# One-core transformer block: the conditioning product moved from TensorE in attention to VectorE multiply-adds under the output projection and the first feed-forward

## The reference

```python
mod = silu(c) @ ada_w + ada_b            # 1024 -> 9216 = 3 sublayers x (shift, scale, gate) x 1024
h = rms_norm(x, g) * (1 + scale) + shift
x = x + 0.5 * gate * swiglu(h)           # sublayer 0, and 2; sublayer 1 has a token mixer and a whole gate
```

## Time and profile before

| | us |
|---|---|
| median of 3 runs | 1898.52 |
| lowest and highest | 1898.12, 1898.67 |
| span of the profiled execution | 1896.2 |
| PE busy | 1868.0 (99%) |
| DVE busy | 996.8 (53%) |
| ACT busy | 817.9 (43%) |
| POOL busy | 123.8 (7%) |

### The profile page before, as it was taken

The page is one execution under the profiler, slowest core; times in us unless marked ns, Lnnn a source line. Parts: engine busy times, 40 slices in busy tenths (PEclk is TensorE's granted clock), DMA queues, the critical chain, the costliest instruction groups (busy, mean ns, idle before and its releaser), DMA issues.

```text
span 1896.2 us, 22387 instructions
## 1 busy us (share of the span) xinstructions
PE 1868.0 (99%) x8923; PEld 1450.5 (76%) x8923; DVE 996.8 (53%) x1778; ACT 817.9 (43%) x1328; POOL 123.8 (7%) x148
## 2 busy tenths in 40 slices
PE   8999999999999999999999999999999999999997
PEld 6566666666788788888886777778888878888886
DVE  6667666666544653333346667845434763333322
ACT  6566656656633342222323655434432442222221
POOL 0111111110001000000010011000000100000000
PEclk9999999999999999999999999999999999999999
DMA  5444343432233232222333323221123323233331
GB/s 199 164 145 156 144 145 145 145 145 101 78 129 117 67 111 100 93 96 94 100 86 125 99 70 106 68 94 35 45 89 111 124 92 102 94 100 97 92 95 61
DMA packets 56526, 201.95 MB, mean 107 GB/s; under 512 B 6478, under 2 KB 6934, under 8 KB 55784
## 3 DMA queue, kind: packets, MB, share of 16 engines
q1 hardware_dynamic: 44616, 158.32, 25.3%
q0 software_dynamic: 11808, 42.21, 6.1%
HBM read 195.23 MB, written 5.28 MB: 106 GB/s over the span
## 4 chain that ended last, share of the span: by engine, by line
PE 87%; DVE 6%; ACT 4%; issue 1%; DMA 0%; SPq 0%; DVEq 0%; ACTq 0%
PE ps L1204 25%; PE ps L1207 24%; PE ps L1205 24%; PE ps L1304 2%; PE ps L1268 2%; PE ps L1340 1%; ACT wH L1910 1%; PE ps L1292 1%; DVE wL L1499 1%; PE ps L1280 1%; ACT a L2009 1%; DVE a L1622 1%; PE ps L1347 1%; PE ps L1257 1%; DVE g1a L1499 1%
## 5 line engine op out<-in xcount | busy, mean ns | idle before, releaser
L1204 PE MATMUL ps<-hH,wH 128*128 128x512 f32 (+1 forms) x1560 | 634.8, 407 | 1.0 <-DVE hL L1570 1.0
L1207 PE MATMUL ps<-hH,wL 128*128 128x512 f32 (+1 forms) x1560 | 610.7, 391 | 1.0 <-DVE wL L1499 0.7
L1205 PE MATMUL ps<-hL,wH 128*128 128x512 f32 (+1 forms) x1560 | 609.0, 390 | 0.0
L1499 DVE TENSOR_TENSOR wL<-wr,wH 128x1024 fp32r<-128x1024 f32 (+2 forms) x285 | 343.9, 1207 | 483.8 <-ACT wH L1910 483.2
L1910 ACT ACTIVATE wH<-wr 128x1024 fp32r<-128x1024 f32 (+2 forms) x285 | 295.1, 1036 | 233.3 <-PE ps L1207 218.3
L1204 PEld LDWEIGHTS ps<-hH,wH 128*128 128x128 f32 (+1 forms) x1560 | 292.7, 188 | 93.6 <-issue 32.4
L1207 PEld LDWEIGHTS ps<-hH,wL 128*128 128x128 f32 (+1 forms) x1560 | 292.3, 187 | 66.9 <-DVE wL L1499 3.9
L1205 PEld LDWEIGHTS ps<-hL,wH 128*128 128x128 f32 (+1 forms) x1560 | 293.1, 188 | 61.3 <-issue 6.5
L1204 PE MATMUL ps<-gffn,wH 128*128 128x512 f32 x400 | 157.0, 393 | 1.0 <-DVE xT L1677 0.9
L1205 PE MATMUL ps<-gffn,wH 128*128 128x512 f32 x400 | 155.8, 390 | 0.0
L1207 PE MATMUL ps<-gffn,wL 128*128 128x512 f32 x400 | 155.8, 390 | 0.0
(11 more groups left out here) (304 smaller groups left out, 2079.9 us busy)
## 6 DMA issues: line engine op xcount, KB each, us to landing
wr<-wst SPq DMA_DIRECT2D x268, 512.0 KB, 3.4
a<-wfd POOLq DMA_DIRECT2D x54, 512.0 KB, 5.0
xT<-wfd POOLq DMA_DIRECT2D x18, 512.0 KB, 6.9
wr<-wst SPq DMA_DIRECT2D x16, 384.0 KB, 3.0
xT<-xin SPq DMA_DIRECT2D x8, 256.0 KB, 6.8
xT<-xin SPq DMA_DIRECT2D x2, 1024.0 KB, 7.0
xsave<-xT SPq DMA_DIRECT2D x1, 2048.0 KB, 7.3
c<-wfd POOLq DMA_DIRECT2D x8, 256.0 KB, 3.7
```

Source lines behind the costliest of these rows:

```text
L1204: e.matmul(o, hi, xh[k], start=k == 0, stop=False)
L1205: e.matmul(o, hi, xl[k], start=False, stop=False)
L1207: i = e.matmul(o, lo, xh[k], start=False, stop=k == t.nk - 1)
L1499: e.tensor_tensor(dst, x, hi.bitcast(F32), ALU.subtract).then_inc(s[name], 1)
```

## The change

The modulation leaves attention and TensorE. DVE now makes it, as multiply-adds: an accumulator of 128x1024 takes a block of ada_w times one column of silu(c) per partition, eight blocks one after another, and one product of PE with a column of ones then sums over the partitions (`fed_sum`). There are five parts p (`FED`: 2, 1, 2, 2 and 2 blocks wide), 72 units in all.

- 24 units (parts 0 and 1, the first sublayer's numbers) stand every third step of the output projection, from step 6 to step 75. The sums stand three steps after the last unit of their part: at step 6 of tile 3 and step 14 of tile 4. POOL issues the first four loads when the last z tile is done, and one more after each unit.
- 48 units (parts 2 to 4) stand in tiles 0 to 23 of the first feed-forward's rest, two at step 3 of each; their sums at step 5 of tiles 8, 16 and 24.
- The stored numbers come back in two transfers (24 rows, later 48), with two turns on PE (`mod` at step 12 of tile 5, `mod2`), and the factors are made for sublayer 0 first (`mod_rest`, now at step 1 of tile 6).
- The raw chunks 0 to 5 move from tiles 4 to 6 to tiles 6 and 7. The shift rows stay.
- PSUM bank 7 joins the ring for small work in attention. The buffers of parts 0 and 1 lie where hH and hL are dead, the later ones where the feed-forward's last six operands come; ACT waits for the last sum before it writes those.

```diff
-NADA = 18
 ADA_BUFS = 4
+FED = [(0, 2), (2, 1), (3, 2), (5, 2), (7, 2)]
+FED_AT = [8 * sum(n for _, n in FED[:p]) for p in range(len(FED))]
...
+    def fed(self, i, end):
+        self.add("fed", i=i, next=i + ADA_BUFS if i + ADA_BUFS < end else None, a2v=self.sig("a2v"))
+    def fed_sum(self, p):
+        self.add("fed_sum", p=p, adm=self.sig("adm"), row=self.sig("row"))
+        self.move("fed_row", p=p)
+    def fed_later(self, i, k):
+        if i < 24 and k == 3:
+            for j in range(2):
+                self.fed(FED_AT[2] + 2 * i + j, len(ADA))
+        if k == 5 and i in (8, 16, 24):
+            self.fed_sum(i // 8 + 1)
+        if k == 1 and i == 27:
+            self.move("fed_mod")
+        if k == 7 and i == 28:
+            self.add("mod2", modt=self.sig("modt"))
...
-        pb, mi, sc = Ring([0, 1]), Ring([6, 5]), Ring([2, 3, 4])
+        pb, mi, sc = Ring([0, 1]), Ring([6, 5, 7]), Ring([2, 3, 4])
...
-            for n in range(NADA):
-                if ada_step(n) // 24 == i:
-                    put(ada_step(n) % 24, ada, n)
...
-        more = {4: [lambda: add("mod_rest"), lambda: self.raw(1, 0), lambda: self.raw(1, 1)],
-                5: [lambda c=c: self.raw(1, c) for c in (2, 3, 4)], 6: [lambda: self.raw(1, 5)], 7: [lambda: self.raw(1, 6)]}
+        more = {7: [lambda: self.raw(1, 6)]}
         at = {(6, 9): lambda: self.shift_row(1, 0, first), (7, 1): lambda: self.shift_row(1, 1, first + 1),
-              (7, 8): lambda: self.shift_row(1, 2, first + 2)}
+              (7, 8): lambda: self.shift_row(1, 2, first + 2), (5, 12): lambda: add("mod", modt=sig("modt")),
+              (5, 4): lambda: self.move("mod_in"), (6, 1): lambda: add("mod_rest")}
+        for step, chunks in ((6, 3), (0, 2)), ((6, 7), (2, 4)), ((6, 12), (4, 5)), ((7, 3), (5, 6)):
+            at[step] = lambda chunks=chunks: [self.raw(1, c) for c in range(*chunks)]
+        add("fed_start", done=self.h_lasts[1], i=0, n=FED_AT[2])
+        fed, sums = {6 + 3 * i: i for i in range(FED_AT[2])}, {}
...
+                if 16 * c + k in fed:
+                    i = fed[16 * c + k]
+                    self.fed(i, FED_AT[2])
+                    if i + 1 in FED_AT:
+                        sums[16 * c + k + 3] = fed_unit(i)[0]
+                if 16 * c + k in sums:
+                    self.fed_sum(sums[16 * c + k])
...
+                elif what == "fed_sum":
+                    p = d["p"]
+                    take(7)
+                    bank_free[7] = ("row", d["row"])
+                    w.wait_ge(s["a2v"], FED_AT[p] + 8 * FED[p][1])
+                    for q in range(2 * FED[p][1]):
+                        acc = fed_views(FED_AT[p] + q // 2)[0]
+                        i = e.matmul(ps[7][32 * q:32 * q + 1, :], C("one", 0, 1), acc[:, 512 * (q % 2):512 * (q % 2) + 512],
+                                     start=True, stop=True)
...
+                elif what == "fed":
+                    i = d["i"]
+                    p, k, j = fed_unit(i)
+                    acc, buf = fed_views(i)
+                    w.wait_ge(s_ada[i % ADA_BUFS], 16 * (i // ADA_BUFS + 1))
+                    if k == 0:
+                        if p > 2:
+                            w.wait_ge(s["adm"], p)
+                        e.tensor_scalar(acc, buf, csil[:, 0:1], None, ALU.mult, ALU.bypass).then_inc(s["a2v"], 1)
+                    else:
+                        w.wait_ge(s["a2v"], i + 1 - FED[p][1])
+                        e.scalar_tensor_tensor(acc, buf, csil[:, k:k + 1], acc, ALU.mult, ALU.add).then_inc(s["a2v"], 1)
...
+                elif what == "fed_start":
+                    w.wait_ge(s["slot"], d["done"])
+                    for i in range(d["i"], d["i"] + ADA_BUFS):
+                        fed_feed(i)
+                elif what == "fed":
+                    if d["next"] is not None:
+                        w.wait_ge(s["a2v"], d["a2v"])
+                        fed_feed(d["next"])
```

More of the change, by code:

```diff
@@ L558, in ffn @@
         self.whole(up(1))
+        if sub == 0:
+            add("fed_start", done=self.h_lasts[1] + 16, i=FED_AT[2], n=len(ADA))
         for j in range(2, 22):
-            self.whole(gate(j))
-            self.whole(up(j))
+            for i, t in enumerate((gate(j), up(j))):
+                for k in self.steps_of(t):
+                    if sub == 0:
+                        self.fed_later(2 * (j - 2) + i, k)
         self.h_lasts[n + 1] = len(self.slots)
@@ L1499, in lo_of, with factors @@
                 e.tensor_tensor(dst, x, hi.bitcast(F32), ALU.subtract).then_inc(s[name], 1)
+            def factors(subs):
+                for sub in subs:
+                    j, a = 24 * sub, gs[:, 8 * sub:8 * sub + 8]
+                    own(e.tensor_scalar(a, mod[:, j + 8:j + 16], 1.0, None, ALU.add, ALU.bypass))
+                    own_done()
+                    e.tensor_tensor(a, a, S("ng", 8 * sub, 8 * sub + 8), ALU.mult)
+                    e.tensor_scalar(gate[:, 8 * sub:8 * sub + 8], mod[:, j + 16:j + 24], 0.5, None,
+                                    ALU.mult, ALU.bypass).then_inc(s["modd"], 1)
+                w.wait_ge(s["modd"], subs[-1] + 1)
             for what, d in steps:
@@ L1679, in _ @@
                     w.wait_ge(s["mod"], 1)
-                    for sub in range(3):
-                        j, a = 24 * sub, gs[:, 8 * sub:8 * sub + 8]
-                        own(e.tensor_scalar(a, mod[:, j + 8:j + 16], 1.0, None, ALU.add, ALU.bypass))
-                        own_done()
-                        e.tensor_tensor(a, a, S("ng", 8 * sub, 8 * sub + 8), ALU.mult)
-                        e.tensor_scalar(gate[:, 8 * sub:8 * sub + 8], mod[:, j + 16:j + 24], 0.5, None,
-                                        ALU.mult, ALU.bypass).then_inc(s["modd"], 1)
-                    w.wait_ge(s["modd"], 3)
+                    factors(range(1))
                 elif what == "out_up":
```

122 lines of the change are left out of this document (56 added, 66 removed).

## The result

The kernel after takes 1911.17 us, median of four runs (1909.94 to 1912.41), against 1898.53 of the kernel before in the same session: ratio 1.0066, 95% interval 1.0052 to 1.0080. So it is slower by 12.6 us. Its profiled span is 1908.9 us.

What follows compares the result with a forecast made beforehand. PE, busy 99%, was taken to bound the kernel, hiding an ACT and DVE loop in attention. -12.4 + 4.7 + 1.4 + 6.7 + 1.7 + 3.3 = +5.4 took the span from 1896.2 to 1901.6; plus 2.3, 1903.9 us, range 1893.5 to 1913.

Steps and rivals of the forecast that it cites:

- attention's gain: Attention: an ACT and DVE loop of about 27.1 us per round limits the gain to 12.4 us, range 10 to 15.
- the load: Projection, fourth slot: POOL's loads delay its weights by 4.3 us, so PE waits and +1.4 us is added.
- the sums: PE's five added sums take at most 4.6 us and the second turn about 0.1: together +4.7 us.
- the first sum's wait: Projection, step 6 of tile 3: PE waits 6.7 us for DVE's units; clock loss counted separately.
- E: Rival, chance 0.15: landing of 8.2 us makes four buffers too few, DVE late at both projection sums; 1912 us.
- Which wait it would be: Attention: PE would wait about 1.5 us or less for DVE at the first turn of each round.
- The second sum: Projection, 24 steps after the first sum: DVE about on time, wait 0 to 1 us.
- Tiles 6 and 7: Projection's end: DVE's 24.1 us of work for 21.8 us of steps makes the last add of x late, +3.3 us.
- the dearer case in the prediction: Projection: full 1.8 us per DVE and POOL meeting, not 1.03, would make the first sum 1.5 us later.
- B: Rival, chance 0.23: fourth slot's load not held up, first sum waits 2.8 us, clock stays; 1896.7 us.
- C: Rival, chance 0.05: ACT and DVE only keep step with PE, rounds become 25.1 us, attention gives 37; 1879.3 us.
- D: Rival, chance 0.07: attention's loop is 26.2 us, as in the last round, and gives 24; 1892.3 us.

Runs made afterwards that it cites:

- e1: The kernel after, with the third block of softmax weights made at step 14 of an attention round, not 16: 1889.6 us, ratio 0.9956.
- e2: The kernel after without the 63 multiply-adds and their loads, only the first of eight blocks of each part multiplied: 1897.8 us, ratio 1.0001.
- e5: The kernel after, with the transfer of x back queued behind the weights of the projection's fourth slot: 1907.4 us, ratio 1.0042.
- e6: The kernel after, with the first sum at step 66 of the projection, not 54: 1907.2 us, ratio 1.0047.
- e7: The kernel after, with part 1's eight units in the feed-forward, first sum at step 60, factors and chunks a tile earlier: 1906.8 us, ratio 1.0045.
- e11: e9 with the feed-forward's first eight units spread over four slots, other parts and all four sums two slots later: 1866.3 us, ratio 0.9831.
- e12: e11 with the first head's first two blocks of weights made at step 14, not 16 and 17: 1864.5 us, ratio 0.9821.
- e4: The kernel before, with the third block of softmax weights made at step 14 of an attention round: 1890.3 us, ratio 0.9959.
- e8: The kernel after with e1, e5 and e7 joined, and the low part of a head's squares made before the split: 1874.1 us, ratio 0.9872.
- e3: The kernel after, with two PSUM banks, not three, in the ring for small work in attention: 1909.5 us, ratio 1.0064.
- e9: e8 with the projection's sum at step 64 and no feed-forward unit ahead of the previous part's sum: 1874.1 us, ratio 0.9873.
- e10: e9 with the first head's scores at steps 14, 19, 23 and weights at 16, 17, 21, 25: 1877.6 us, ratio 0.9886.

## Why the prediction held in range and sign, and where its sum was off

The forecast was 1903.9 us, slower, within 1893.5 to 1913.0; measured were 1911.17. That lies in the range, but above the forecast's own bounds (1899 to 1909): the sum was +5.4 us, and the profiled spans differ by +12.7. The steps that failed were sizes: attention's gain was taken 3.0 us too large, the load 2.7 too small and the sums 1.7 too small. They outweighed the first sum's wait, which was taken 1.6 too long. One chance was also added up wrongly: two thirds of 0.50 and E's 0.15 are 0.48 for slower, not 0.56. By its steps, each against the table of pairs:

- **Attention, predicted -12.4, measured -9.44.** The mechanism is right and shown by e1: a loop of 27.1 us (it is 27.18) that PE's shorter queue can't touch. The size was off by 3.0, in terms that can be read from the starts of the first turns. Round 3's is at 92.91 and not 92.6 (0.3), although the waits at the first head grew by 3.7 us (4.26 + 1.66 against 2.19). The period is 0.08 longer, 1 us over 12 rounds. And one round is 28.7 us long (1.6): the clock is at 0.81 in its window. The last takes 26.3, and 26.2 was said. The long round is this execution's event: e2, e5, e6 and e7 have the same attention, with one, one, two and no such rounds, and it gives 9.1, 9.2, 8.9 and 11.9 us there. So some 3 us of this term differ from one execution to the next, and the 12.4 lie above all of them.
- **Which wait it would be** was half right. The turn waits 0.35 us, and the larger one of 1.40 stands 2 us later, at the sum for a head's output (L1291), whose operand DVE makes behind the split. I had read only the turn as the place where the loop meets PE.
- **Sums, predicted +4.7, measured 6.4.** In e11 a sum of four products (8 records) adds 1.19 us and one of two (4 records) 1.18, so what counts is a sum and not its records; I had divided the 1.83 us of 16 records. The second turn adds 0.42 and not 0.1. Five sums and the turn are 6.4 us at full clock.
- **The load, predicted +1.4, measured +4.09.** The load came 5.2 us later (4.3 predicted) and the waits are 1.9 us. Of the rest, 2.2 us, some 1.5 is half clock: e6 has the same waits with the clock at 1.00 and loses 2.6. The step that failed: I gave the clock a price behind the long wait only. It isn't a fixed price either, as the same 1.4 us of wait in attention cost nothing in 13 rounds of 14.
- **The first sum, predicted 6.7, its own 0.9 and 1.7 of half clock behind it, measured 8.19.** The wait is 5.09 us; the sum's own 1.19 and 1.9 of half clock are the rest. DVE's count was right: its last unit of part 0 ended at 592.7, 46.6 us behind the projection's start, and 45.5 was predicted. The wait is shorter only because PE itself came 2.9 us later than thought, most of it by the load: what the load's term had too little, this one had in part too much. A POOL add of 1.44 us, at 583.64, made a group of three units take 4.70 us where three others took 3.8. This is the block between two readers of SBUF that the Trainium skill describes (SBUF — State Buffer, "Who interferes with whom"); the trace has 0.9 us for it, not the full 1.8 of the dearer case in the prediction.
- **The second sum, 0 to 1 and its own 0.9, measured 2.42**: a wait of 0.90, the sum's own 1.18, and 0.4 of the first turn, which stands here now. The wait is right, and the clock behind it stayed.
- **Tiles 6 and 7, predicted +3.3, measured +3.41**, and for the reason given, as e2 and e7 show. The split is a little different, and that the sum fits so well is in part luck: the wait grew by 1.8 us (2.3 predicted), and 1.6 are half clock, which came in after and not in e6.
- **The feed-forward, 0**: right but for the sums' own price. No wait for DVE or for a load is there.
- Rivals: B fell with the late weights and the wait at the first sum. C and D fell with the 27.18 us. E gave 1912, nearly the measured time, and is still wrong: DVE waited for loads of ada_w 1.3 us in the whole projection, so four buffers were enough. That a rival's number is right says nothing without its mark in the trace.

The rule of the Trainium skill on the clock (TensorE: Matmul & The Clock Gate, "What's actually happening"), that it follows how busy PE has recently been, decided less in attention than it might have: 1.7 us of wait in each round of 27 left the clock at 1.00, as in the window from 202 us, in all rounds but one of after.

**What the change could have given.** With the loop shortened by 1.8 us in two places, one transfer moved, one part put where DVE is free, and each sum put behind DVE's real pace, the same idea takes 1866.3 us (e11) or 1864.5 us (e12): 0.9821 of the kernel before, 34 us under it and 47 under the kernel after. Attention is shorter by 38.5 to 40.6 us there, about the 38.7 us of PE's work that left it, and 6.7 are paid behind it. But not all of that is the moved product's: the one entry of the table gives 7 to 8 us without it (e4, 0.9959). Against e4, e11 and e12 are 24 to 26 us shorter, and the loop's other edit, the squares' low part made earlier, has no run on the kernel before. What is left of waits in e12 is 5.1 us in the first heads, 6.4 at the start before the first products, and 5 elsewhere.

## What to carry to other kernels

Before work is taken off the engine that is busy 99%, measure the period of the others with that engine's waits left out. Here 27.1 us against 26.9 said that little of 38 us would come at first (9.4 did). The idle gap of 4 us in DVE's queue, behind an instruction that waits although the next one could run, was where another 21 lay. Work that is moved to an engine with free time needs a schedule by that engine's own backlog, place by place: an average of half a queue free hides that it comes out of one stage 8 us behind, and a sum that stands too early on the main engine is paid with the wait and again with the clock. Move a wait's place only after asking whether the backlog behind it is gone, since otherwise it comes back at the next meeting point, as in the run with the first sum later.

## What the runs showed of the hardware

- The granted clock doesn't follow the length of a wait alone. Waits of 0.35 and 1.40 us, 2 us apart, left it at 1.00 in 13 rounds of one execution and halved it in one (0.81 in that window of 9 us, products at 0.43 us distance and not 0.23). 1.38 and 0.53 us behind the late weights brought half clock in after and cost 4.09 us in all; in e6 like waits cost 2.6. Longer waits did both too: 2.19 us at the first head of before brought it (0.52), 2.46 at e8's first sum and 2.70 at the start of e6's feed-forward did not (1.00 over the 3.5 and 8.5 us behind). 5.09 us and more brought it wherever they stood (after, e1, e3, e5, e6, e9, e10). I found no rule for which case comes.
- The time at which the clock first rose to full differs: in the records of the fourteen profiled executions it is between 10.6 (e12) and 15.3 us (e11), and the products behind come earlier or later by half of the difference, up to 2.4 us of a span.
- Four transfers of 0.5 MB, and a fifth 5 us later, issued on POOL's queue with 2 MB of SP's made a third transfer, queued behind SP's, 5.2 us later; three made it 3.3 us later (e2). At the 365 GB/s of the earlier trace rows the 5.2 us are 1.9 MB, nearly all four. How the two queues shared isn't settled by it.
- A multiply-add of 128x1024 on DVE takes 1.28 us where nothing holds it up (80.3 us for 63 of them is 1.27 from start to start, blocks and all counted); the estimate from narrower ones was 1.24.
- A sum over the partitions by products with a column of ones has one price, 1.18 to 1.19 us, for two products of 512 columns as for four (e11).
